# Every projection in three reduced-precision passes, with most of the weight splitting moved to GpSimd

## The chip, the core and the metric

The kernel runs on one core of one Trainium2 chip. The metric is device time in microseconds (us) of one execution. TensorE (PE in the profile) multiplies, VectorE (DVE) and ScalarE (ACT) do elementwise work, GpSimd (POOL) is a slower elementwise engine, SyncE (SP) issues the DMAs. Each engine works through its own instructions in program order and waits on semaphores that the others raise.

## The reference

Two layers of a backbone act on 128 context tokens and 128 latent tokens (width 1024, float32). Cut to what matters here:

```
h = rmsnorm(x) * (1 + scale) + shift                 # adaLN modulation from silu(c) @ w_ada
z = h @ w_in                                         # conv_in, conv_gate, ssm_in, ssm_gate, q, k, v, attn_gate, merge
A) ya = a * sigmoid(g); depthwise conv, 31 taps; layernorm; silu;   br_a = (ya * silu(conv_gate)) @ w_conv_out
B) yb = bidirectional complex state space scan (32 groups, state 64);
   yg = gelu(yb) @ w_ssm_glu; yb = yg_a * sigmoid(yg_b);            br_b = (yb * silu(ssm_gate)) @ w_ssm_out
C) q, k = rmsnorm per head, rotary for the latent tokens; o = softmax(q k / 8) v
                                                                    br_c = (o * silu(attn_gate)) @ w_attn_out
mixed = sigmoid(m_a) * br_a + sigmoid(m_b) * br_b + sigmoid(m_c) * br_c
x = x + gate * (mixed @ w_out)
```

Outputs are both token streams after two layers, the context keys and values of each layer, and the final scan states.

## The kernel before

The two token streams (s = 0 context, s = 1 latent) each fill the 128 partitions. A projection of up to 512 columns is a "unit". Its weights come in slabs of two 128-row tiles (512 KB for 512 columns) through a ring of seven buffers called `raw`, and one slab means 2 streams x 2 tiles = 4 products of 128x128 by 128x512. Units of `w_in`: `cg`, `ssm`, `ca` (early), `q`, `kv` (256 columns), `sg`, `ag` (this group is called the zone here), `gg` (run inside attention), `glub` and `glua` (the state space GLU, inside attention too), the merge gates `meB0` to `meA1`, then branch outputs `brB0` to `brA1` and `wo0`, `wo1`.

A unit is computed in one of two ways. The plain way (`plain_slab`, line 805) multiplies in full float32. The split way (`split_products`, lines 833 to 835) writes a weight as a high part plus a low part in the type fp32r, and does three cheaper products: high by high, high by low, low by high. The high part of a slab (a "piece") is a ScalarE copy of 1024 elements per partition into a spare room (line 1193), the low part is a VectorE subtraction raw - high (`low_parts`, through the helper at line 1477) written back over `raw`. Before the change `cg`, `ssm`, `ca`, all merge, branch and output units are split, and `q`, `kv`, `sg`, `ag`, `gg`, `glub`, `glua` are plain.

The order of the work is written out by hand in `order(l)`, and all engines follow the same list of stages. For each layer, in words:

- early units, then `UT`, `S` (states in, PE L963), `cp` (VectorE computes the scaled matrix CP, 12 operations of 1024 elements), `bbar`, `bz` (GpSimd), the zone units with `K` between them.
- `scan`: VectorE runs 32 dependent steps, each of four additions or products of 128 elements. Behind it on VectorE: `qkn` (squares, norm, rotary of q and k), some convolution taps, then the copies `HY<-H` for which the stage `Y` on PE (L1053, L1055) waits.
- `conv`: 31 x 4 = 124 taps per layer, each one VectorE operation on 256 elements (line 1584), handed out by `TAPS_IN_ZONE`, `TAPS_IN_ATT` and the `conv` stages. The last tap has to be done before `cback` behind the sixth of the merge units (`comb C 0`).
- attention `att 0`, `att 1` with `gg`, `glub`, `glua` pieces between the steps; then six `comb` stages B0, B1, C0, C1, A0, A1, each four merge pieces and two branch pieces; then `wout`.

In layer 0 the stages `comb A` also hold `pre` for the next layer: VectorE computes 12 operations of 1024 elements there (`tA<-lamc,bbar` and the like).

PSUM has four `proj` banks used in turn, so a unit waits until the bank four uses back is drained.

Of the kernel before, what the change touches and what calls it, by code (L numbers as in the profile page):

```python
# [47 lines left out]
EARLY = ("cg", "ssm", "ca")  # L48
LATE_ROOMS = 3
# [6 lines left out]
IN_ATT_UNITS = ("gg", "glub", "glua")  # L56


def order(l):

    def nxt(*stage):
# [4 lines left out]
             ("chunks", "ca", 4), ("pre", 0, 1), ("unit", "ca"), ("taps", 0), ("preE", 0, 0), ("pack",), ("preE", 0, 1)]  # L66
    if l:
# [4 lines left out]
    turn = [] if l else [("bbar", l)]  # L72
    return (begin
            + [("UT",), ("S",), ("cp",)] + turn + [("bz", 0), ("convT", 0), ("convT", 1), ("unit", "q"), ("unit", "kv"),
               ("adaE", l, 2), ("K", 0), ("unit", "sg"), ("bz", 1), ("K", 1), ("unit", "ag")] + nxt("adaE", n, 0)
            + [("scan", 0, NCHUNK), ("qkn",), ("conv", TAPS_IN_ZONE[l], None), ("Y",), ("adaT", l, 2)] + nxt("adaT", n, 0)
            + [("qkT", 0), ("qkT", 1), ("att", 0)] + nxt("adaE", n, 1)
            + [("geT",), ("att", 1), ("unit", "glub"), ("unit", "glua"), ("split", 0), ("split", 1)]
            + nxt("adaT", n, 1)
            + [("brT", "B", 0), ("brT", "B", 1), ("conv", 12, "B0"), ("comb", "B", 0)]  # L80
            + nxt("bT", n) + [("brT", "C", 0), ("brT", "C", 1), ("conv", 12, "B1"), ("comb", "B", 1)]
            + nxt("cT", n) + [("conv", -1, "C0"), ("comb", "C", 0)]
# [47 lines left out]
def stages():  # L130
    out = [(0, s) for s in (("cond",), ("ada", 0, 0, 0, 2), ("small",), ("tabA",), ("mod",), ("ada", 0, 0, 2, DT),
                            ("sq", 0, 0), ("sq", 0, 1), ("xn", 0, 0), ("xn", 0, 1), ("adaE", 0, 0), ("adaT", 0, 0),
                            ("tabS",), ("hT", 0, 0), ("hT", 0, 1), ("early", 0, 0), ("early", 0, 1),
                            ("ada", 0, 1, 0, DT), ("adaE", 0, 1), ("adaT", 0, 1), ("hT", 1, 0), ("hT", 1, 1),
                            ("early", 1, 0), ("chunks", "cg", 1), ("early", 1, 1))]
    for l in range(DEPTH):
        out += [(l, s) for s in order(l)]
    return out
# [16 lines left out]
def split_unit(u):  # L155


    return u[:2] in ("me", "br", "wo") or u in EARLY

# [87 lines left out]
def build(nc, A, C, O):  # L247

    with ExitStack() as ctx:  # L249
# [29 lines left out]
        mixed, mixeds = shared("mixed", [P, NS, D])  # L279
        y2 = mixed[:, :, 0:W]  # L280
        ytok = mixed[:, :, W:D]
        hT = sb("hT", [P, NS, DT, P])
# [7 lines left out]
        pre = sb("pre", [P, 2, 16, L, GC])  # L290
# [3 lines left out]
        tA = sb("tA", [P, 1024])  # L294
        tB = sb("tB", [P, 1024])
        brows = tA[:, :].rearrange("x (p c) -> x p c", p=SP)
        bz = sb("bz", [P, 2, 16, 3 * GC])
        bbar = sb("bbar", [P, 2, G, GC])
# [18 lines left out]
        geT = HYf[:, 0, :].rearrange("p (s t q) -> p s t q", s=NS, t=WT)  # L317
# [15 lines left out]
        th = sb("th", [P, 4, W])  # L333

# [13 lines left out]
        hTs = high_low(Hs, DT)  # L348
# [72 lines left out]
        pieces = [key for key in order_of_slabs if key[0] != "ada" and split_unit(key[1])]  # L421
        piece_at = {key: m for m, key in enumerate(pieces)}
        piece_hi = sem("piece_hi")
        piece_lo = sem("piece_lo")
# [9 lines left out]
        rooms_of = lambda u: early_room if u in EARLY else wout_room if u[:2] == "wo" else late_room  # L434
        piece_room, piece_prev, n_of, last_in = [], [], {}, {}
        for m, (l, u, kp) in enumerate(pieces):
            kind = "early" if u in EARLY else "wout" if u[:2] == "wo" else "late"
            i = n_of.get((l, kind), 0) % len(rooms_of(u))
            n_of[(l, kind)] = n_of.get((l, kind), 0) + 1
            where = ("early" if kind == "early" else "late", i)  # L440
            piece_room.append(rooms_of(u)[i])
            piece_prev.append(last_in.get(where))
            last_in[where] = m

        def piece_slot(m, tile):
            n = KT_SLAB * W * (slab_at[pieces[m]] % RAW)
            return tile[:, n:n + KT_SLAB * W]

        def piece_raw(m):
            return raw[:, slab_at[pieces[m]] % RAW, :]  # L450

        def ahead(l, u, beside=2):

            m = max(i for i, c in enumerate(pieces) if c[:2] == (l, u)) + 1
            room = 0 if m == len(pieces) or (pieces[m][1] in EARLY) != (u in EARLY) else beside
# [8 lines left out]
        for key, _, _, _ in slabs:  # L464
            if key[0] != "ada" and split_unit(key[1]):
# [4 lines left out]
            elif key[0] == "ada":  # L470
                ring = ada_ring(key[:3])
                slab_read.append((ring.full, ring.at[key[:3]][0] + 1))
            else:
                slab_read.append((proj.full, proj.at[key[:2] + (NS - 1,)][0] + 1))
# [12 lines left out]
        split_lo = sem("split_lo")  # L487
# [45 lines left out]
        qk_rs = sem("qk_rs")  # L533
        qk_done = sem("qk_done")
# [45 lines left out]
        for l, stg in todo:  # L580
            if stg[0] in ("split", "brT"):
# [43 lines left out]
        def _(sp):  # L625
# [26 lines left out]
            def b_loads(l):  # L652
                if l:
                    sp.wait_ge(cp_done, 2 * l)
                    sp.wait_ge(bbar_done, l)
                for d in range(2):
                    for r, nm in enumerate(("ssm_b_re", "ssm_b_im")):
                        sp.dma_start(tA[64 * d + 32 * r:64 * d + 32 * r + 32, :],
                                     A[nm][l, d].rearrange("g p c -> g (p c)")).then_inc(b_in, 16)

            def mid_loads(l):
# [3 lines left out]
                if l:  # L665
                    sp.wait_ge(prodA, NS * l)
                    sp.wait_ge(gelu_done, NS * l)
                    sp.wait_ge(qk_done, NS * l)
                    sp.wait_ge(long_.full, long_.at[("pv", l - 1, 1)][0] + 1)
# [7 lines left out]
            def results(l):  # L677
                sp.wait_ge(qk_done, ls(l, 0))
# [81 lines left out]
        def _(pe):  # L760
# [30 lines left out]
            def plain_slab(key):  # L791

                l, u, kp = key
                nk, n = nk_of(u), cols_of(u)
                lhs = geT if u[:2] == "gl" else hT
# [3 lines left out]
                slab_landed(pe, key)  # L799
                w = slab_view(key)  # L800
                for s in range(NS):
                    for i in range(KT_SLAB):
                        kt = KT_SLAB * kp + i
                        last = kt == nk - 1
                        m = T.matmul(proj.bank((l, u, s))[:, 0:n], lhs[:, s, kt, :], w[:, i, :],  # L805
                                     start=(kt == 0), stop=last)
                    if last:
                        m.then_inc(proj.full, 1)
                if not last:
                    m.then_inc(slab_used, 1)  # L810

            def slab_work(key):
                if key[0] == "ada":
                    ada_slab(key)
                else:
                    plain_slab(key)
# [5 lines left out]
            def split_products(l, u, kt, lhs, streams):  # L822
# [4 lines left out]
                part = slice(W * (kt % KT_SLAB), W * (kt % KT_SLAB) + W)  # L827
                pe.wait_ge(piece_lo, m_ + 1)
                whi, wlo = piece_room[m_][:, part], piece_slot(m_, raws)[:, part]
                for s in streams:  # L830
                    bank = proj.bank((l, u, s))
                    hi, lo = (lhs[i][:, s, kt % WT if u[:2] == "wo" else kt, :] for i in range(2))
                    T.matmul(bank[:, :], hi, whi, start=(kt == 0), stop=False)  # L833
                    T.matmul(bank[:, :], hi, wlo, start=False, stop=False)  # L834
# [1257 lines left out]
```

## Time and profile before

| | us |
|---|---|
| median of 3 runs | 714.88 |
| lowest, highest | 713.8, 714.9 |
| the profiled execution | 713.04 |
| its span | 711.0 |
| its mean granted TensorE clock | 0.969 |

Busy time in the span: PE 652.4 us, DVE 551.5, ACT 297.3, POOL 36.4. The span is what the instruction records cover, and the execution's own time is 2.04 us longer. Busy shares are averages; the stage tells which engine holds the others up.

### The profile page before, as it was taken

Reading aid. Unit: us, or ns where it says so; the run is one execution under the profiler, and the core shown is the slowest. Engines: PE = TensorE matmul, PEld = TensorE weight load, DVE = VectorE, ACT = ScalarE, POOL = GpSimd, SP = SyncE. Lnnn points to the kernel's source line nnn. Section 1 sums busy time; section 2 is a strip of 40 time slices with the busy share of each in tenths; the row PEclk is TensorE's granted clock in tenths of the full one; section 3 lists DMA queues with packets and bytes.
Section 4 is the critical chain, followed back from the end, with each engine's and each line's share of the span. In section 5 each row is a group of like instructions: output and inputs, shape, how many; then the busy total and the mean of one; then the engine's idle time right before and its main releaser. Section 6 shows DMA issues by size and latency. Waiting matters only on the chain. (4 is left out here: it accounts for less than half of the span.)

```text
span 711.0 us, 9584 instructions
## 1 busy us (share of the span) xinstructions
PE 652.4 (92%) x3573; PEld 466.5 (66%) x3573; DVE 551.5 (78%) x1024; ACT 297.3 (42%) x454; POOL 36.4 (5%) x49
## 2 busy tenths in 40 slices
PE   3689899996997999998999899999897999999997
PEld 1368674553843688877887687465664578877885
DVE  3679689989777886589975657998878698887663
ACT  2564350212533445435455736011445444436441
POOL 2100001111000000010001010012000000010000
PEclk9989889998998999999999999999998999999999
DMA  8992817654383274654543437660632346655631
GB/s 289 348 275 70 275 36 232 239 183 141 123 272 122 75 229 146 179 176 149 167 158 95 138 136 252 205 240 11 198 112 66 89 121 184 199 165 164 201 104 59
DMA packets 67305, 117.65 MB, mean 165 GB/s; under 512 B 11052, under 2 KB 15484, under 8 KB 67260
## 3 DMA queue, kind: packets, MB, share of 16 engines
q1 hardware_dynamic: 66980, 116.94, 51.9%
q8 instruction: 28, 0.46, 0.3%
q10 hardware_dynamic: 280, 0.11, 0.1%
q14 instruction: 17, 0.14, 0.1%
HBM read 112.51 MB, written 1.38 MB: 160 GB/s over the span
## 5 line engine op out<-in xcount | busy, mean ns | idle before, releaser
L805 PE MATMUL proj<-raw,hT 128*128 128x512 f32 (+1 forms) x320 | 132.0, 558 | 0.0
L1584 DVE SCALAR_TENSOR_TENSOR cvacc<-cvpad,taps,cvacc 128x256 f32<-128x256 f32 x240 | 98.6, 477 | 0.3
L805 PEld LDWEIGHTS proj<-raw,hT 128*128 128x128 f32 x320 | 58.2, 190 | 58.8 <-issue 57.0
L1477 DVE TENSOR_TENSOR raw_split<-raw,wide_split 128x1024 fp32r<-128x1024 f32 x56 | 67.9, 1220 | 21.6 <-ACT wide_split L1193 20.9
L1193 ACT ACTIVATE wide_split<-raw 128x1024 fp32r<-128x1024 f32 x56 | 58.6, 1059 | 55.9 <-PE proj L835 55.9
L834 PE MATMUL proj<-raw_split,H_split 128*128 128x512 f32 x192 | 75.4, 393 | 0.0
L833 PE MATMUL proj<-wide_split,H_split 128*128 128x512 f32 x144 | 57.9, 402 | 4.7 <-DVE raw_split L1477 4.7
L835 PE MATMUL proj<-wide_split,H_split 128*128 128x512 f32 x144 | 56.9, 395 | 0.0
L1477 DVE TENSOR_TENSOR raw_split<-raw,utok_split 128x1024 fp32r<-128x1024 f32 x28 | 34.2, 1220 | 15.1 <-ACT utok_split L1193 15.1
L1193 ACT ACTIVATE utok_split<-raw 128x1024 fp32r<-128x1024 f32 x28 | 29.6, 1058 | 34.8 <-PE proj L835 34.8
L834 PEld LDWEIGHTS proj<-raw_split,H_split 128*128 128x128 f32 x192 | 36.4, 190 | 7.3
L1477 DVE TENSOR_TENSOR H<-H,qkt 128x128 f32<-128x128 f32 x128 | 39.0, 305 | 2.2
L834 PE MATMUL proj<-raw_split,mixed_split 128*128 128x512 f32 x96 | 38.5, 401 | 0.0
L834 PE MATMUL proj<-raw_split,qM_split 128*128 128x512 f32 x96 | 37.5, 391 | 0.0
L833 PEld LDWEIGHTS proj<-wide_split,H_split 128*128 128x128 f32 x144 | 27.5, 191 | 11.9 <-DVE raw_split L1477 4.7
L805 PE MATMUL proj<-raw,HY 128*128 128x512 f32 x64 | 32.4, 653 | 0.0
L835 PEld LDWEIGHTS proj<-wide_split,H_split 128*128 128x128 f32 x144 | 27.4, 190 | 5.9
L1390 ACT ACTIVATE pre<-side,nmx 128x128 f32<-128x128 f32 (+1 forms) x32 | 13.2, 416 | 41.2 <-PE side L820 16.4
L1166 ACT ACTIVATE gates<-proj 128x512 f32<-128x512 f32 x12 | 7.0, 597 | 54.7 <-PE proj L805 54.7
L1053 PE MATMUL side<-qM,Uz 128*64 128x64 f32 x128 | 19.7, 239 | 8.4 <-DVE HY L1908 8.4
L1055 PE MATMUL side<-EC,HY 128*64 128x64 f32 x256 | 25.4, 237 | 0.0
L834 PE MATMUL proj<-raw_split,HY_split 128*128 128x512 f32 x64 | 24.9, 390 | 0.0
(252 smaller groups left out, 1327.0 us busy)
## 6 DMA issues: line engine op xcount, KB each, us to landing
raw<-in_w_in SPq DMA_DIRECT2D x104, 512.0 KB, 4.3
raw<-in_w_ada SPq DMA_DIRECT2D x48, 512.0 KB, 5.3
raw<-in_w_out SPq DMA_DIRECT2D x16, 512.0 KB, 3.8
raw<-in_w_ssm_glu SPq DMA_DIRECT2D x8, 512.0 KB, 7.0
raw<-in_w_ssm_out SPq DMA_DIRECT2D x8, 512.0 KB, 4.3
raw<-in_w_attn_out SPq DMA_DIRECT2D x8, 512.0 KB, 3.7
raw<-in_w_conv_out SPq DMA_DIRECT2D x8, 512.0 KB, 3.7
raw<-in_w_in SPq DMA_DIRECT2D x8, 256.0 KB, 3.7
```

The source lines that it names most:

```text
L805: m = T.matmul(proj.bank((l, u, s))[:, 0:n], lhs[:, s, kt, :], w[:, i, :], start=(kt == 0), stop=last)
L833: T.matmul(bank[:, :], hi, whi, start=(kt == 0), stop=False)
L834: T.matmul(bank[:, :], hi, wlo, start=False, stop=False)
L835: m = T.matmul(bank[:, :], lo, whi, start=False, stop=last)
L1053: T.matmul(o, Uz[:, g, :], M[:, :, g // 2, :], start=True, stop=False)
L1055: m = T.matmul(o, HY[:, q % 2, gi, r, :, :].rearrange("p s k -> p (s k)"), CP[:, r, 1:L + 1, g, :], start=False, stop=(r == 1))
L1166: S.activation(gates[:, GATE[u], s, :], proj.bank(key)[:, :], ACT.Silu).then_inc(proj.freed(key), 1)
L1193: S.activation(piece_room[m], piece_raw(m), ACT.Copy).then_inc(piece_hi, 1)
L1390: m = S.activation(prob[:, p % 2, nk * P * a:nk * P * a + nk * P], side.bank(key)[:, nk * P * a:nk * P * a + nk * P], ACT.Exp, bias=nmx[:, ...
L1477: return V.tensor_tensor(out, a, b, op)
L1584: m = V.scalar_tensor_tensor(acc, src, taps[:, t, j:j + 1], acc, ALU.mult, ALU.add)
```

## The change

All units become split. The low parts are shared out by `low_on_pool`: GpSimd subtracts for the zone units, for the units inside attention, and for the merges B0, B1, C0, A0 and A1; VectorE keeps those of the early units, of C1 and of `wout`. That the activations are now kept as a high and a low copy for the whole layer (`hTe`) removes the `split` stages from attention. Further moves: `bbar` and the norm and rotary of k go to GpSimd, the sums of squares to ScalarE (`sumsq`, 20 small activations a layer), the norm of q into the scale of the exponential, the copies `HY<-H` ahead of q's norm, and convolution taps from the zone and attention to the merges.

```
-def split_unit(u):
-    return u[:2] in ("me", "br", "wo") or u in EARLY
+def low_on_pool(u):
+    return u in ZONE or u in IN_ATT_UNITS or u[2:] in ("B0", "B1", "C0", "A0", "A1")
...
-TAPS_IN_ZONE = (16, 8)
-TAPS_IN_ATT = (((8, 8, 8, 8, 8), (7, 4, 4, 7, 0)), ((6, 6, 6, 6, 6), (7, 4, 4, 7, 0)))
+TAPS_IN_ZONE = (4, 0)
+TAPS_IN_Y = (0, 4, 6)
+TAPS_IN_ATT = (((8, 8, 5, 5, 2), (5, 5, 5, 5, 0)), ((6, 6, 3, 3, 2), (5, 5, 5, 5, 0)))
...
-            + [("UT",), ("S",), ("cp",)] + turn + [("bz", 0), ("convT", 0), ("convT", 1), ("unit", "q"), ("unit", "kv"),
-               ("adaE", l, 2), ("K", 0), ("unit", "sg"), ("bz", 1), ("K", 1), ("unit", "ag")] + nxt("adaE", n, 0)
-            + [("scan", 0, NCHUNK), ("qkn",), ("conv", TAPS_IN_ZONE[l], None), ("Y",), ("adaT", l, 2)] + nxt("adaT", n, 0)
+            + [("UT",), ("S",), ("cp",), ("bz", 0), ("convT", 0), ("convT", 1), ("unit", "q"), ("unit", "kv"), ("adaE", l, 2),
+               ("sumsq", 0), ("K", 0), ("bz", 1), ("unit", "sg"), ("sumsq", 1), ("K", 1), ("scan", 0, NCHUNK), ("HY",),
+               ("unit", "ag")] + nxt("adaE", n, 0)
+            + [("qkn",), ("conv", TAPS_IN_ZONE[l]), ("Y",), ("adaT", l, 2)] + nxt("adaT", n, 0)
...
-            + [("brT", "B", 0), ("brT", "B", 1), ("conv", 12, "B0"), ("comb", "B", 0)]
-            + nxt("bT", n) + [("brT", "C", 0), ("brT", "C", 1), ("conv", 12, "B1"), ("comb", "B", 1)]
-            + nxt("cT", n) + [("conv", -1, "C0"), ("comb", "C", 0)]
+            + [("brT", "B", 0), ("brT", "B", 1), ("conv", 22), ("comb", "B", 0)]
+            + nxt("bT", n) + [("brT", "C", 0), ("brT", "C", 1), ("conv", 22), ("comb", "B", 1)]
+            + nxt("cT", n) + [("conv", -1), ("comb", "C", 0)]
...
                 for m in range(lows[0], upto):
-                    dve.wait_ge(piece_hi, m + 1)
-                    tt_(piece_slot(m, raws), piece_raw(m), piece_room[m].bitcast(F32),
-                        ALU.subtract).then_inc(piece_lo, 1)
+                    if not low_on_pool(pieces[m][1]):
+                        dve.wait_ge(piece_hi, m + 1)
+                        tt_(piece_slot(m, raws), piece_raw(m), piece_high(m).bitcast(F32),
+                            ALU.subtract).then_inc(piece_lo[0], 1)
...
+            def low_parts(upto):            # GpSimd's
+                for m in range(lows[0], upto):
+                    if low_on_pool(pieces[m][1]):
+                        pool.wait_ge(piece_hi, m + 1)
+                        tt_(piece_slot(m, raws), piece_raw(m), piece_high(m).bitcast(F32),
+                            ALU.subtract).then_inc(piece_lo[1], 1)
```

First place, GpSimd from the zone on, layer 0. Before:

```order
L2039 MEMSET bz 128x1536
L2040 COPY bz<-bbar 64x32x16
L2041 COPY bz<-bbar 64x32x16
L2042 COPY bz<-bbar 128x32x16
L2040 COPY bz<-bbar 64x32x16
L2041 COPY bz<-bbar 64x32x16
L2042 COPY bz<-bbar 128x32x16
L2005 TENSOR_SCALAR qst<-qst 128x10
```

The same place with the change (`raw_split<-raw,..._split` is a low part, 1024 elements for a full piece and 512 for one of `kv`):

```order
L2111 COPY bz<-bbar 128x32x16
L2007 TENSOR_TENSOR raw_split<-raw,pre_split 128x1024 x2
L2007 TENSOR_TENSOR raw_split<-raw,gates_split 128x1024
L2007 TENSOR_TENSOR raw_split<-raw,pre_split 128x512 x2
L2007 TENSOR_TENSOR raw_split<-raw,gates_split 128x512
L2007 TENSOR_TENSOR raw_split<-raw,pre_split 128x512
L2007 TENSOR_TENSOR raw_split<-raw,pre_split 128x1024
L2007 TENSOR_TENSOR raw_split<-raw,gates_split 128x1024
L2109 COPY bz<-bbar 64x32x16
```

GpSimd, which had three copies at a time here, now has the low parts of all sixteen zone pieces, twelve full ones and four half ones, around those copies.

Second place, VectorE through the merges B0 and B1, layer 0. Before (a tap is `cvacc<-cvpad,taps,cvacc`):

```order
L1972 SCALAR_TENSOR_TENSOR HY_split<-side,HY_split 128x512 x2
L1584 SCALAR_TENSOR_TENSOR cvacc<-cvpad,taps,cvacc 128x256 x4
L1477 TENSOR_TENSOR raw_split<-raw,wide_split 128x1024
L1584 SCALAR_TENSOR_TENSOR cvacc<-cvpad,taps,cvacc 128x256 x4
L1477 TENSOR_TENSOR raw_split<-raw,wide_split 128x1024
L1584 SCALAR_TENSOR_TENSOR cvacc<-cvpad,taps,cvacc 128x256 x4
L1477 TENSOR_TENSOR raw_split<-raw,utok_split 128x1024
L1477 TENSOR_TENSOR raw_split<-raw,wide_split 128x1024 x2
L1947 SCALAR_TENSOR_TENSOR mixed<-th,proj 128x512
```

With the change, as far as the end of C0's taps:

```order
L1978 SCALAR_TENSOR_TENSOR HY_split<-side,HY_split 128x512 x2
L1609 TENSOR_SCALAR cvacc<-cvpad,taps 128x256 x2
L1612 SCALAR_TENSOR_TENSOR cvacc<-cvpad,taps,cvacc 128x256 x20
L1953 SCALAR_TENSOR_TENSOR mixed<-th,proj 128x512 x2
L1978 SCALAR_TENSOR_TENSOR qM_split<-side,qM_split 128x512 x2
L1612 SCALAR_TENSOR_TENSOR cvacc<-cvpad,taps,cvacc 128x256 x22
L1953 SCALAR_TENSOR_TENSOR mixed<-th,proj 128x512 x2
L1612 SCALAR_TENSOR_TENSOR cvacc<-cvpad,taps,cvacc 128x256 x18
```

The low parts are gone from VectorE's list, and 62 taps stand where 28 stood (74 for 46 in layer 1).

## Rows read from the trace of the kernel before

**Rows 1.** Page, part 1: busy us (share) and instructions.

```profile
PE 652.4 (92%) x3573; PEld 466.5 (66%) x3573; DVE 551.5 (78%) x1024; ACT 297.3 (42%) x454; POOL 36.4 (5%) x49
```

**Rows 2.** Timeline of PE, layer 1's zone: start, us, engine, line.

```profile
457.34 1.99 PE L805 MATMUL proj<-raw,hT 128*128 128x256 f32 x8
...
471.87 14.00 PE L805 MATMUL proj<-raw,hT 128*128 128x512 f32 x32
...
490.36 14.00 PE L805 MATMUL proj<-raw,hT 128*128 128x512 f32 x32
507.34 0.45 PE L1053 MATMUL side<-qM,Uz 128*64 128x64 f32 x2 [2.98 <-DVE HY L1908]
```

**Rows 3.** Timeline of PE, a split unit, twelve products apart.

```profile
596.86 0.39 PE L833 MATMUL proj<-utok_split,H_split 128*128 128x512 f32 x1
...
599.58 0.39 PE L833 MATMUL proj<-wide_split,H_split 128*128 128x512 f32 x1
```

**Rows 4.** Timeline of DVE, layer 1's zone.

```profile
440.96 1.23 DVE L1477 TENSOR_TENSOR tA<-cT,lamr 128x1024 f32<-128x1024 f32 x1
...
455.72 0.29 DVE L1477 TENSOR_TENSOR qkt<-H,lamI 128x128 f32<-128x128 f32 x1
...
490.82 0.83 DVE L1477 TENSOR_TENSOR qkt<-qk 128x640 f32<-128x640 f32 x1 [0.33 <-DVE H L1477]
...
506.17 1.97 DVE L1908 COPY HY<-H 64x1024 f32<-64x1024 f32 x2
```

**Rows 5.** Timeline of DVE, layer 0's zone.

```profile
115.03 1.29 DVE L1477 TENSOR_TENSOR tA<-bbar,coef 128x512 f32<-128x512 f32 x2
...
131.73 0.58 DVE L1477 TENSOR_TENSOR qkt<-H,lamI 128x128 f32<-128x128 f32 x1
...
133.83 0.29 DVE L1477 TENSOR_TENSOR qkt<-H,lamI 128x128 f32<-128x128 f32 x1
```

**Rows 6.** Timeline of POOL: copies beside that scan; a one-element operation.

```profile
131.47 0.69 POOL L2040 COPY bz<-bbar 64x512 f32<-64x512 f32 x1 [9.09 <-PE side L976]
132.22 0.76 POOL L2041 COPY bz<-bbar 64x512 f32<-64x512 f32 x1
133.04 0.61 POOL L2042 COPY bz<-bbar 128x512 f32<-128x512 f32 x1
...
636.14 1.07 POOL L2005 TENSOR_SCALAR st<-st 128x1 f32<-128x1 f32 x1 [5.07 <-DVE st L1919]
```

**Rows 7.** Timeline of DVE at that one-element operation.

```profile
635.97 1.19 DVE L1477 TENSOR_TENSOR raw_split<-raw,wide_split 128x1024 fp32r<-128x1024 f32 x1
```

**Rows 8.** Groups of instructions on POOL by line, shapes apart: busy, mean ns.

```profile
L2014 POOL COPY qk<-ldt 64x128 f32<-64x128 f32 x1 | 0.3, 282 | 9.0 <-DMA ldt<-in_ssm_log_dt 9.0
```

**Rows 9.** Timeline of PE, layer 0: stage Y begins.

```profile
174.93 0.44 PE L1053 MATMUL side<-qM,Uz 128*64 128x64 f32 x2 [5.44 <-DVE HY L1908]
```

**Rows 10.** Timeline of PE, first attention of layer 1.

```profile
522.85 3.60 PE L805 MATMUL proj<-raw,hT 128*128 128x512 f32 x8
...
526.93 3.60 PE L805 MATMUL proj<-raw,hT 128*128 128x512 f32 x8
```

**Rows 11.** Timeline of DVE, there: six taps.

```profile
523.58 2.46 DVE L1584 SCALAR_TENSOR_TENSOR cvacc<-cvpad,taps,cvacc 128x256 f32<-128x256 f32 x6
```

**Rows 12.** Windows: length, busy of PE, PEld, DVE, ACT, POOL, clock, DMA.

```profile
247.00:303.60 56.60, 56.60 (x298) 46.95 (x298) 40.76 (x61) 25.28 (x29) 0.00 (x0) 0.97 0.62 191
...
574.00:624.00 50.00, 49.95 (x224) 41.37 (x225) 45.25 (x75) 22.27 (x25) 0.00 (x0) 1.00 0.59 175
```

**Rows 13.** Windows, PE alone: layer 0's merges A0 and A1.

```profile
324.00:362.00 38.00, 36.04 (x172) 1.00 0.54 163
```

**Rows 14.** Groups on ACT by line: high parts, small evictions.

```profile
L1193 ACT ACTIVATE wide_split<-raw 128x1024 fp32r<-128x1024 f32 x56 | 58.6, 1059 | 55.9 <-PE proj L835 55.9
...
L1377 ACT ACTIVATE wide<-side 48x160 f32<-48x160 f32 x32 | 7.7, 290 | 10.9 <-PE side L976 10.9
```

More of the change, by code:

```diff
@@ L152, in units_of, with kind_of @@
     return []
-def split_unit(u):
-    return u[:2] in ("me", "br", "wo") or u in EARLY
+def kind_of(u):
+    if u in EARLY:
+        return "early"
+    if u in ZONE:
+        return "zone"
+    if u in IN_ATT_UNITS:
+        return "att"
+    return "wout" if u[:2] == "wo" else "late"
+def low_on_pool(u):
+    return u in ZONE or u in IN_ATT_UNITS or u[2:] in ("B0", "B1", "C0", "A0", "A1")
 def side_uses(l, stage):
@@ L464, in build @@
         for key, _, _, _ in slabs:
[L465 removed]
+            if key[0] != "ada":
                 slab_read.append(piece_read[piece_at[key]])
@@ L580, in build @@
         for l, stg in todo:
-            if stg[0] in ("split", "brT"):
+            if stg[0] == "geT":
+                parts += [(l, "geT", s) for s in range(NS)]
+            elif stg[0] == "brT":
                 parts.append((l,) + stg)
@@ L798, in plain_slab @@
                         proj.claim(pe, (l, u, s))
[L799 to L816, printed above, removed]
+                for kt in range(KT_SLAB * kp, KT_SLAB * kp + KT_SLAB):
+                    split_products(l, u, kt, geTs if u[:2] == "gl" else hTe, range(NS))
             def transpose(out, in_):
@@ L1102, in _ @@
                     for u, nk, n in units_of(stg):
-                        if not split_unit(u):
+                        if k == "unit" and u not in EARLY:
                             for key in slab_keys(l, stg):
@@ L1313, in _ @@
                 elif k == "unit" and stg[1] in ("sg", "ag"):
+                    high_parts(ahead(l, stg[1]))
                     gate(l, stg[1])
+                elif k == "sumsq":
+                    s = stg[1]
+                    proj.drained(act, (l, "q", s))
+                    proj.drained(act, (l, "kv", s))
+                    for i in range(HEADS + KV):
+                        h = i // 2 + 4 * (i % 2) if i < HEADS else i
+                        m = S.activation(sq_out[:, s, HD * i:HD * i + HD], qk[:, s, HD * i:HD * i + HD], ACT.Square,
+                                         accum_out=qst[:, s, 0, h:h + 1])
+                    m.then_inc(qk_sq, 1)
                 elif k == "comb":
@@ L2025, in _ @@
                     for s in range(NS):
-                        pool.wait_ge(qk_sq, ls(l, s))
-                        rsqrt_mean(qst[:, s, 2, :], qst[:, s, 0, :], HD, HEADS + KV, qst[:, s, 1, :], qk_rs)
+                        k_norm(l, s)
+                elif k == "UT":
+                    low_parts(piece_at[(l, "q", 1)])
+                elif k == "unit" and stg[1] in ZONE:
+                    low_parts(ahead(l, stg[1]))
+                elif k == "HY":
+                    low_parts(ahead(l, "ag"))
+                elif k == "att":
+                    low_parts(ahead(l, "glua" if stg[1] else "gg"))
+                elif k == "comb":
+                    low_parts(ahead(l, "br" + stg[1] + str(stg[2]), 0))
+                elif k == "bbar":
+                    pool.wait_ge(pre_done, 2 * (l + 1))
+                    pool.wait_ge(tab_done, 1)
+                    if l:
+                        side.filled(pool, ("K", l - 1, 7))
+                    for i in range(2):
+                        side.drained(pool, ("bT", l, i))
+                    co = [coef[:, j, G * l:G * l + G].unsqueeze(2).to_broadcast([P, G, GC]) for j in range(2)]
+                    t0, t1 = (bzf[:, W * i:W * i + W].rearrange("p (g c) -> p g c", g=G) for i in range(2))
+                    b0, b1 = (bbar[:, r, :, :] for r in range(2))
+                    tt_(t0, b0, co[1])
+                    link(tt_(t1, b1, co[1]))
+                    tt_(b0, b0, co[0])
+                    link(tt_(b1, b1, co[0]))
+                    tt_(b0, b0, t1, ALU.subtract)
+                    tt_(b1, b1, t0, ALU.add).then_inc(bbar_done, 1)
                 elif k == "cback":
```

330 lines of the change are left out of this document (175 added, 155 removed).

## The prediction

> **What bounds the kernel now.** I read the busy shares first. TensorE is busy for 92% of the span, VectorE for 78%, ScalarE for 42%, GpSimd for 5% [rows 1]. So TensorE is the first suspect, and GpSimd is nearly free. Then I read TensorE's timeline stage by stage, to see which stages are really its own. In layer 1's zone it runs without a hole from 471.87 to 504.36, then stands for 2.98 us until 507.34, and what releases it is VectorE's copy `HY<-H` [rows 2]. In layer 0 the same hole is 5.44 us, up to 174.93 [rows 9]. VectorE's timeline shows why: the scaled matrix from 440.96, the scan from 455.72 to 490.5, then q's and k's norm, taps, and the copies only at 506.17 [rows 4]. The zone is thus nearly balanced, with VectorE last. In the merges B0 to C0 TensorE is busy all the time: 56.6 of 56.6 us in layer 0 and 49.95 of 50.00 in layer 1, with VectorE at 45.25 of the 50 in layer 1 [rows 12]. Again two engines close together, TensorE ahead.
>
> **What TensorE saves.** Four plain slabs take 14.00 us, so one takes 3.50 [rows 2]. A split slab is twelve products, 599.58 - 596.86 = 2.72 us [rows 3]. That is 0.78 us less per slab, and there are 20 full ones in a layer (q, sg, ag, gg four each, glub and glua two each): 15.6 us. A `kv` slab of 256 columns takes 1.99 us [rows 2]. Split products of that width are not in the trace, and with half of 2.72 they would take 1.36, with no gain at all 1.99. I take 1.4, so 2.4 us for four. Together 18 us a layer, 36 us in all: the profiled execution's 713.04 could become 677 and no less, if everything else kept up.
>
> **What GpSimd's part costs.** The change puts 50 full and 4 half subtractions a layer on GpSimd, which did none. The question is what VectorE does meanwhile. Layer 0's scan shows it: steps take about 1.05 us (34.8 us less the delay below, over 32 steps [rows 4]), but the one that begins at 131.73 takes 2.10 [rows 5], while three GpSimd copies of 512 elements run [rows 6]. 1.05 us over three copies is 0.35 us of delay for each. And the other way: a GpSimd operation on one element, at 636.14, takes 1.07 us and ends just behind VectorE's subtraction of 635.97, which takes 1.19 us [rows 6, 7]. So each holds the other off when both read two SBUF streams or one against two. The Trainium skill says so in "SBUF — State Buffer", section on who shares ports: the pair is an exclusive lock, held for the full instruction, and a VectorE operation with two SBUF inputs contends with a GpSimd one that reads SBUF. The trace agrees on the two cases above. It speaks against this change: every scan step, every tap and the scaled matrix have two SBUF inputs.
>
> How long a subtraction of 1024 elements holds VectorE is not in the trace; call it p. Lower end: counting elements alone, twice a copy's 512 at 0.35, 0.70 us. Scaled by both inputs, 2 x 2 x 0.35 = 1.4. Upper end: four times a copy's own undisturbed 0.61 [rows 6], 2.44. A copy of 128 elements takes 0.282 [rows 8] and one of 512 takes 0.61, so 0.33 us for 384 more, 0.86 ns an element: 2048 elements read make 1.76 us. I take p = 1.76, since it comes from two rows on GpSimd's own rate with the fixed part out, and keep 0.7 and 2.44 for the range. A half piece costs p/2.
>
> The skill has a price for it, in "GPSIMD Engine Reference", section 3.1: a two-input addition of 2048 fp32 elements takes 4497 ns, so as an estimate 2.25 us for 1024. By that price the sum below would be +41 us in place of +8, some 756 us.
>
> **The zone, part by part.** Off VectorE's chain before `Y` go the norm, rotary and taps between 490.5 and 506.17 [rows 4]; they move behind the copies, where `Y` (from 507.34 to about 520) covers them, and the k part to GpSimd. In layer 0 `bbar` goes too: the scan can begin at 115.2 instead of 119.0 [rows 5]. Added on GpSimd beside the scaled matrix and the scan are q2, q3, the four half pieces, sg and ag: ten full and four half, 12p. (TensorE reaches ag at about 482, before the scan ends, so all of them fall inside it.) The `bz` copies are in the measured scan already. From the scan's end to `Y` I take 2.0 us, ScalarE's copy of the forward half. Layer 1: Y at 490.5 + 12p + 2.0 = 492.5 + 21.1 = 513.6 for 507.34 before, **+6.3**. TensorE's own work would be done at 504.4 - 12 x 0.78 - 2.4 = 492.6, so it waits 21 us for the scan. Layer 0: 115.2 + 34.8 + 21.1 + 2.0 = 173.1 for 174.93, **-1.8**.
>
> **Attention.** In layer 1 a step took 4.08 us [rows 10], of which the taps are 2.46 [rows 11]. With five or so taps (2.05) and about 1.05 of reductions and copies VectorE needs 3.1 + p = 4.9, +0.8 for each of four steps. At the end of the first attention twelve taps become two, 10 x 0.41 = 4.1 us less on the chain. In the second the two splits of the activations go, about 1. Together -2 in layer 1; in layer 0 its longer steps (5.3, with two adaLN slabs in each) cover p, so -3. **-5**.
>
> **The merges.** B0, B1, C0 are 18 pieces. VectorE loses 18 subtractions, but has 74 taps in layer 1 (46 before) and 62 in layer 0 (28 before), 0.41 us each by [rows 11], and all need two SBUF inputs. The last tap must precede `cback`, which ends the stage. GpSimd can do three pieces ahead, as there are three rooms, so the two share 15p + 74 x 0.41 + 1.4 (two additions) = 26.4 + 30.3 + 1.4 = 58.1 us where TensorE took 50.0 [rows 12]: **+8.1**. In layer 0: 26.4 + 25.4 + 1.4 = 53.2, hidden under 56.6: 0. While VectorE is late its `mixed` operations free the branch banks late, and that is where TensorE will stand. A0 and A1 in layer 0: 12p + twelve operations of `pre` at 1.23 + 2.8 = 38.6 us against 38.0 [rows 13], so 0. In layer 1 A0 and A1 have no `pre`, and p is below a piece's 2.72: 0.
>
> ScalarE gains 22 full copies at 1.06 us (four of `kv` at half), and 20 sums of squares a layer, by the nearest small operation 0.29 each, 6 us [rows 14]. At 42% busy it has room: 0, or +4 if a copy stands before an exponential.
>
> **Sum** for p = 1.76: +6.3 - 1.8 - 5 + 8.1 = +7.6 us on the profiled execution's 713.04, that is 720.6. That execution lies 1.8 under the median of the runs, 714.88; on the median it is 722.5, and I say 722. The steps move with p by 12 in each zone, 8 in each attention and 15 in layer 1's merges, so some 50 us per us of p, and no change lies at p = 1.6.
>
> **Rivals.**
> - *TensorE's gain comes through.* If GpSimd's reading leaves gaps that VectorE uses (p = 1.4 or less). For it: the delay measured is only 0.35 of a copy's 0.61. Against: two inputs. At 1.4: +2.0 - 6.1 - 8 + 2.7 = -9.4, 705 us. At 0.7: -6.4 - 14.5 - 13 + 0 = -34, 681 us, near the floor of 36.
> - *The lock for the full instruction* at 2.1 to 2.44: layer 1's zone +14.5, layer 0's +6.4, merges +18.3 and +6.8, A0 and A1 +8.7 at the upper end, 770 us; at 2.1 some 745. For it: the one-element operation that waited the whole of VectorE's. It decides above p = 1.6, as the forecast does, only more so. Its place is layer 1's scan: a hole on TensorE of over 25 us.
> - *No difference.* p between 1.55 and 1.65, 712 to 717.
> - *ScalarE sets the pace* in attention and gives 4 to 8 us of a gain back: 710, if p is 1.4. Against it: its idle time there.
>
> **Chances.** Forecast (p 1.65 to 1.95) 0.31, all slower. Full lock 0.19, slower. Gain comes through 0.37, faster; ScalarE rival 0.05, faster. No difference 0.08. A measurement of this kernel tells 0.2% from nothing. So faster 0.42, same 0.08, slower 0.50. The range goes from 686 (p about 0.85) to 746 (p about 2.1). The forecast's own is 715 to 731.
>
> **What would show it.** Slabs of 2.72 us with L847 to L849 in the zone: the saving is there. The GpSimd subtraction's mean, and VectorE's scan: 34.8 us before, about 52 with p = 1.76. The start of `Y` against 507 - 441. TensorE idle before L1053's successor, released by `HY`. Taps whose mean is far above 477 ns in B0 to C0. I am wrong if the scan stays under 45 us, and then the time is near 700; I am wrong the other way if a subtraction takes 2.2 us and all of it is seen in the scan.

## The result, and the profile after

The changed kernel takes 777.5 us (775.8 to 779.7, 4 runs) against 714.3 (709.0 to 714.9, 4 runs): ratio 1.090 [1.084, 1.096], so 9% slower. The forecast was 722 with a range of 686 to 746. Direction right, size wrong. The rival of the full lock (770) comes nearest. The profiled execution took 779.66 us, its span is 777.9.

Page of the changed kernel, busy us by engine, and the chain that ended last; the first row answers to [rows 1]:

```profile
PE 642.9 (83%) x3765; PEld 508.0 (65%) x3765; DVE 619.9 (80%) x936; ACT 348.5 (45%) x578; POOL 340.4 (44%) x189
...
DVE 50%; PE 31%; issue 4%; ACT 4%; SPq 4%; DMA 4%; POOL 2%; ACTq 0%; DVEq 0%; POOLq 0%
```

VectorE has 88 instructions fewer than before and is busy for 68 us more. It now carries half of the chain. TensorE's stages, by the starts of `S`, `Y` and `cback` in both traces (before / after, us):

| stretch | layer 0 | layer 1 |
|---|---|---|
| S to Y | 84.8 / 89.6 | 74.9 / 89.5 |
| Y to cback | 128.9 / 142.3 | 116.7 / 135.2 |
| cback to next S, or end | 128.6 / 143.5 | 86.9 / 88.2 |

TensorE's timeline in layer 1's zone answers to [rows 2]. The first rows open four split slabs; they take 517.26 - 506.02 = 11.24 us, so 2.81 each where a plain one took 3.50. The last is the hole ahead of `Y`, 2.98 us before:

```profile
506.02 0.50 PE L847 MATMUL proj<-pre_split,hTh 128*128 128x512 f32 x1
506.36 0.39 PE L848 MATMUL proj<-raw_split,hTh 128*128 128x512 f32 x1
...
517.26 2.97 PE L990 MATMUL side<-EC,bz 128*48 128x80 f32 x40
...
554.48 0.45 PE L1069 MATMUL side<-qM,Uz 128*64 128x64 f32 x2 [21.16 <-DVE HY L1642]
```

VectorE's timeline there answers to [rows 4]: two instructions of the scaled matrix, the first alone and the second beside GpSimd, the copy ahead of the scan, the first multiplication of the scan, its last additions, and the copies that release `Y`:

```profile
476.19 1.23 DVE L1508 TENSOR_TENSOR HY<-cT,lamr 128x1024 f32<-128x1024 f32 x1
...
479.84 3.30 DVE L1508 TENSOR_TENSOR HY<-cT,lamr 128x1024 f32<-128x1024 f32 x1
...
499.10 2.39 DVE L1852 COPY H<-h 128x128 f32<-128x128 f32 x1
501.52 2.34 DVE L1508 TENSOR_TENSOR qkt<-H,lamI 128x128 f32<-128x128 f32 x1
...
551.62 0.61 DVE L1508 TENSOR_TENSOR H<-H,qkt 128x128 f32<-128x128 f32 x2
...
552.37 1.96 DVE L1642 COPY HY<-H 64x1024 f32<-64x1024 f32 x2
```

The same instruction takes 1.23 us alone and 3.30 beside GpSimd; a multiplication that took 0.29 takes 2.34. From the start of the scaled matrix to the scan's end are 552.2 - 476.2 = 76.0 us, where before 490.5 - 441.0 = 49.5. VectorE's busy time contains this waiting. In layer 0 one such meeting can be read on both engines. VectorE and then GpSimd:

```profile
126.11 0.29 DVE L1508 TENSOR_TENSOR qkt<-H,lamI 128x128 f32<-128x128 f32 x1
...
126.52 2.78 DVE L1508 TENSOR_TENSOR H<-H,qkt 128x128 f32<-128x128 f32 x2
129.34 0.29 DVE L1508 TENSOR_TENSOR qkt<-H,lamI 128x128 f32<-128x128 f32 x1
```

```profile
126.48 2.35 POOL L2007 TENSOR_TENSOR raw_split<-raw,gates_split 128x1024 fp32r<-128x1024 f32 x1 [0.49 <-ACT gates_split L1214]
```

The two additions, 0.61 us otherwise, begin 0.04 us behind the subtraction and end 0.47 behind its end. Groups of the changed kernel, GpSimd's largest, and VectorE's taps and scan additions (477 and 305 ns before):

```profile
L2007 POOL TENSOR_TENSOR raw_split<-raw,wide_split 128x1024 fp32r<-128x1024 f32 x40 | 111.9, 2811 | 59.2 <-ACT wide_split L1214 58.9
```

```profile
L1612 DVE SCALAR_TENSOR_TENSOR cvacc<-cvpad,taps,cvacc 128x256 f32<-128x256 f32 x240 | 157.6, 726 | 0.2
L1508 DVE TENSOR_TENSOR H<-H,qkt 128x128 f32<-128x128 f32 x128 | 56.2, 439 | 2.2
```

Windows of B0 to C0, layers 0 and 1, answer to [rows 12]:

```profile
251.72:321.50 69.78, 61.61 (x303) 50.05 (x301) 52.04 (x76) 26.05 (x31) 41.91 (x16) 0.90 0.55 165
624.35:689.65 65.30, 53.88 (x226) 43.38 (x225) 65.09 (x85) 23.92 (x27) 42.96 (x16) 0.92 0.49 145
```

In layer 1 VectorE is busy for 65.1 of 65.3 us: it sets the pace, where TensorE did. The granted clock fell from 1.00 to 0.92, and the low stretches lie behind TensorE's new waits.

### The profile page after: what moved, and what is told of

It is laid out like the page before. It is cut to its first block, busy times and chain, and to the rows that moved or that the text cites. A ratio compares the mean times of both kernels' runs of the same rounds, so it can differ in the third digit from the quotient of the medians.

```text
span 777.9 us, 10189 instructions
## 1 busy us (share of the span) xinstructions
PE 642.9 (83%) x3765; PEld 508.0 (65%) x3765; DVE 619.9 (80%) x936; ACT 348.5 (45%) x578; POOL 340.4 (44%) x189
## 4 chain that ended last, share of the span: by engine, by line
DVE 50%; PE 31%; issue 4%; ACT 4%; SPq 4%; DMA 4%; POOL 2%; ACTq 0%; DVEq 0%; POOLq 0%
DVE cvacc L1612 15%; DVE qkt L1508 7%; PE proj L847 7%; DVE H L1508 7%; PE proj L849 6%; PE proj L848 6%; DVE HY L1508 6%; DMA raw<-in_w_in 3%; PE side L833 3%; PE side L1071 2%; DVE EC L1508 1%; PE side L977 1%; DVE H L1792 1%; SPq L724 1%; PE side L1069 1%
## 5 line engine op out<-in xcount | busy, mean ns | idle before, releaser
L848 PE MATMUL proj<-raw_split,hTh 128*128 128x512 f32 (+1 forms) x448 | 175.1, 391 | 0.0
L1612 DVE SCALAR_TENSOR_TENSOR cvacc<-cvpad,taps,cvacc 128x256 f32<-128x256 f32 x240 | 157.6, 726 | 0.2
L2007 POOL TENSOR_TENSOR raw_split<-raw,wide_split 128x1024 fp32r<-128x1024 f32 x40 | 111.9, 2811 | 59.2 <-ACT wide_split L1214 58.9
L848 PEld LDWEIGHTS proj<-raw_split,hTh 128*128 128x128 f32 x448 | 86.3, 193 | 15.6
L847 PE MATMUL proj<-wide_split,hTh 128*128 128x512 f32 x144 | 61.1, 424 | 9.9 <-POOL raw_split L2007 7.1
L2007 POOL TENSOR_TENSOR raw_split<-raw,pre_split 128x1024 fp32r<-128x1024 f32 (+1 forms) x20 | 48.7, 2443 | 39.8 <-ACT pre_split L1214 39.8
L849 PE MATMUL proj<-wide_split,hTl 128*128 128x512 f32 x144 | 59.3, 412 | 0.0
L2007 POOL TENSOR_TENSOR raw_split<-raw,utok_split 128x1024 fp32r<-128x1024 f32 x20 | 53.8, 2692 | 2.0 <-ACT utok_split L1214 1.9
L847 PE MATMUL proj<-gates_split,hTh 128*128 128x512 f32 (+1 forms) x112 | 45.1, 402 | 6.4 <-DVE raw_split L1508 4.4
L849 PE MATMUL proj<-gates_split,hTl 128*128 128x512 f32 (+1 forms) x112 | 43.0, 384 | 0.0
```

The costliest lines, as they stand in the source:

```text
L847: T.matmul(bank[:, 0:n], hi, whi, start=(kt == 0), stop=False)
L848: T.matmul(bank[:, 0:n], hi, wlo, start=False, stop=False)
L849: m = T.matmul(bank[:, 0:n], lo, whi, start=False, stop=last)
L1612: m = V.scalar_tensor_tensor(acc, src, taps[:, t, j:j + 1], acc, ALU.mult, ALU.add)
L2007: return Q.tensor_tensor(out, a, b, op)
```

## The experiments

Three theories. **T1, sharing:** a GpSimd subtraction holds VectorE off for its length. **T2, supply:** GpSimd is just too slow for TensorE. **T3, order:** the moved taps, the order and ScalarE's added work. All times are medians; the kernel before took 713.0 to 714.3 in every group.

**GpSimd writes and reads nothing.** The subtraction at line 2021 becomes

```
slot = piece_slot(m, raws).bitcast(F32)
link(Q.memset(slot, 0.0))
link(Q.memset(slot[:, 0:W], 0.0))
Q.memset(slot, 0.0).then_inc(piece_lo[1], 1)
```

> In place of each subtraction GpSimd writes zeros into the same slot two and a half times over: no input is read, the duration stays near that of a subtraction (about 2.4 us). The low parts are left out of the result; nothing else changes. Theory 1 (a GpSimd instruction with two inputs in SBUF holds off VectorE's instructions of the same sort for its whole length): the time falls from 777 to about 690 (680 to 705), the scan of layer 0 from 50.9 to about 35 us, a tap from 726 to about 480 ns. Theory 2 (GpSimd is too slow to feed TensorE, 2.4 to 2.8 us a piece against 2.7): stays at 770 to 780. Theory 3 (the moved taps, the order and the added work on ScalarE): stays at 770 to 780.

The short form keeps only the last write.

> In place of each subtraction GpSimd writes zeros into the slot once, about 0.9 us; the low parts are left out of the result. Theory 1: within 8 us of the kernel with the long writes (about 685). Theory 2: clearly below the kernel with the long writes, near 700, while that one stays near 775. Theory 3: both near 775.

Measured: 704.4 us with the long writes, 702.5 with the short. So 73 of the changed kernel's 777.5 us go by taking away GpSimd's reads at the same length of work (0.95 + 0.53 + 0.96 us for the 2.43 of a subtraction). Making that work 1.5 us shorter for each piece gives about 2 more, inside the scatter of the short form (699.0 to 706.4). T2 is out, and T3 alone cannot explain it. The writes also leave TensorE zeros to multiply by. That this is not what gives the time back is seen in VectorE's rows below, and in the granted clock, 0.97 here and in the kernel before, which multiplies by real low parts. The page of the kernel with long writes, and its chain; VectorE is busy for 154 us less with the same 936 instructions:

```profile
PE 628.5 (90%) x3765; PEld 499.5 (71%) x3765; DVE 465.9 (66%) x936; ACT 348.5 (50%) x578; POOL 313.5 (45%) x405
...
PE 64%; ACT 8%; DMA 7%; DVE 7%; SPq 6%; issue 4%; POOL 3%; ACTq 0%; DVEq 0%; POOLq 0%
```

Its groups: taps and scan are back at the old means.

```profile
L1612 DVE SCALAR_TENSOR_TENSOR cvacc<-cvpad,taps,cvacc 128x256 f32<-128x256 f32 x240 | 97.5, 479 | 0.2
L1508 DVE TENSOR_TENSOR H<-H,qkt 128x128 f32<-128x128 f32 x128 | 38.3, 299 | 2.2
```

The time lies inside the expected 680 to 705, but 14 us above the 690 at its centre. That is a loss of its own, taken up below.

**Where the sharing costs.** Long writes for one group of pieces only (`kind_of(...) == "late"`, and the reverse).

> The changed kernel, GpSimd writing zeros in the same time in place of the subtractions of the merges alone (those low parts are left out of the result); in the zone and the attention it subtracts. Theory 1: of the 73 us between the changed kernel and the one with writes alone, the merges' part comes back: B0 to C0 of layer 1 from 65 to 50 us, 777 to about 735 (730 to 745). If the zone carries the loss: 760 or more.

> The other half: writes in place of the subtractions of the zone and the attention (those low parts are left out of the result), subtractions in the merges. Theory 1: the zones' part comes back, 777 to about 745 (735 to 755), the scans at 35 us. The two parts should add up to about 73 us if the stages are independent.

Measured: 740.5 (37.0 us back) and 747.0 (30.5 back), together 67.5 of the 73. T1's expectations hold for both, and the stages are nearly independent. With writes in the merges alone, TensorE's windows of B0 to C0 are:

```profile
249.37:310.45 61.08, 57.21 (x303) 47.15 (x301) 34.37 (x78) 26.07 (x31) 39.11 (x49) 0.97 0.65 194
601.93:651.91 49.98, 49.98 (x228) 41.42 (x226) 38.97 (x87) 22.89 (x26) 39.45 (x49) 1.00 0.59 176
```

Layer 1 is back at its old 50.0 us. Layer 0 keeps 4.2 us over the 56.9 from its first product to `cback` before, so there the sharing cost 8.7 of 12.9.

**The price by itself, in the kernel before.** In GpSimd's program, beside the scan:

```
+ if k == "scan":
+     pool.wait_ge(h0_done, l + 1)
...
+     for n in range(6):
+         tt_(spare, x[:, 0, :], x[:, 1, :], ALU.subtract).then_inc(beside, 1)
+         pool.wait_ge(beside, 6 * l + n + 1)
```

`spare` is a buffer that is free then, and the last line makes each one wait for the one before it.

> The kernel before, with six subtractions of 1024 elements on GpSimd in each layer beside the scan (two inputs in SBUF, output into a buffer that is free then); no result uses them. Theory 1 (a GpSimd instruction with two inputs holds VectorE's instructions of this sort off for its whole length): each costs the scan about 2.0 to 2.4 us, the scan of layer 0 grows from 35.9 to 48 to 50 us, the kernel by 15 to 28. The prediction's price of 1.76: 10.6 us a scan, at most 20. Theory 2 or 3: nothing, 713.

> The same six places with a copy of 1024 elements, one input in SBUF (about 1.2 us each). Theory 1, if what counts is the two inputs: the scan grows by less than 1 us. Rival (any GpSimd instruction that reads SBUF holds VectorE off for its length): 6 x 1.2 = 7 us a scan, kernel up by 7 to 14.

> The same six places with a write of zeros of 1024 elements, no input (0.9 us each). Theory 1: scan unchanged, 713. Rival (sharing by any access): 6 x 0.9 = 5 us a scan.

Measured: 741.1, 723.1 and 712.2 us. The scans (35.88 and 34.77 us before) took 48.74 and 47.66 beside the subtractions, 40.64 and 39.52 beside the copies, 35.91 and 34.80 beside the writes. So a subtraction costs 2.14 and 2.15 us, a copy 0.79 each time, a write 0.01 at most. Theory 1 holds for the subtraction. For the copy my form of it (only two inputs count) failed: one read input is enough. The rival's 7 to 14 us for the kernel was right (9.3), its 7 us a scan was too much (4.8). VectorE's timeline of the first:

```profile
134.55 2.36 DVE L1478 TENSOR_TENSOR qkt<-H,lamI 128x128 f32<-128x128 f32 x1
136.83 0.28 DVE L1478 TENSOR_TENSOR qkt<-H,lamR 128x128 f32<-128x128 f32 x1
137.04 4.88 DVE L1478 TENSOR_TENSOR H<-H,qkt 128x128 f32<-128x128 f32 x2
141.95 2.44 DVE L1478 TENSOR_TENSOR qkt<-H,lamI 128x128 f32<-128x128 f32 x1
```

GpSimd's groups of the first and of the second kernel:

```profile
L2003 POOL TENSOR_TENSOR cvacc<-x 128x1024 f32<-128x1024 f32 x12 | 29.2, 2432 | 0.8
```

```profile
L2018 POOL COPY cvacc<-x 128x1024 f32<-128x1024 f32 x12 | 13.2, 1098 | 0.6
```

The reader is to see turns: the first multiplication waits for one whole GpSimd instruction, the two additions for two (4.88). The second multiplication, `lamR`, passes in 0.28 us. It needs no result of its forerunner, but that alone does not save it, as two rows of the changed kernel show:

```profile
510.93 2.39 DVE L1508 TENSOR_TENSOR qkt<-H,lamI 128x128 f32<-128x128 f32 x1
513.24 2.48 DVE L1508 TENSOR_TENSOR qkt<-H,lamR 128x128 f32<-128x128 f32 x1
```

There GpSimd's next subtraction begins at 513.13, ahead of `lamR` at 513.24, and `lamR` waits 2.2 us for it. Above, each subtraction waits for the one before it, and the next begins at 136.84, together with `lamR`. In these rows, the one that is clearly ahead goes first, and `lamR` passes where both begin together.

**Cut in four.** In the changed kernel `for j in range(0, o.shape[-1], 256)` around the subtraction of each piece; in the old one 24 subtractions of 256 elements in place of the six.

> The changed kernel with each subtraction of 1024 elements on GpSimd as four of 256. If what a subtraction costs VectorE is its whole length however it is cut: 777 within 3 us. If the two engines take turns instruction by instruction, then VectorE gets an instruction in between each two quarters (0.6 us) and waits a quarter of the time for each: 745 to 765, the scan of layer 0 at 42 to 47 us in place of 50.9.

> The kernel before with 24 subtractions of 256 elements a layer beside the scan, in place of six of 1024 (741 us). Whole length however it is cut: 741 within 2 us. Turns by instruction: the scan grows by less than the 12.5 us of the six long ones, by 7 to 10; the kernel at 728 to 735.

Measured: 778.2 in the changed kernel (no change), 736.6 in the old (741.1 uncut). There the scan took 47.87 and 46.73 us, 12.0 over before in both layers, for 24 quarters of 0.776 us: 0.50 each, 2.0 for four against 2.14 uncut. VectorE gets an instruction in between, but the quarters' own time grows: four of 0.776 are 3.1 us against 2.43. In the changed kernel a quarter takes 0.83 to 0.94 us, and the scans grew to 53.5 and 54.2 us where turns were to give 42 to 47. Its stages moved both ways, `Y` to `cback` of layer 1 from 135.2 to 128.4 us and the last stretch from 88.2 to 96.5; why was not looked into. The first theory's number was right for the changed kernel; for the old one neither was (it asked for 741 within 2, the other for a scan 7 to 10 longer).

**The merges' subtractions on VectorE.** `low_on_pool` without B0 to A1, and behind every fourth tap `low_parts(lows[0] + 1)`, as before; then only A0 and A1.

> The subtractions of all merges (B0, B1, C0, A0, A1) go back to VectorE, those of B0 to C0 between its taps as in the kernel before; the zone's and the attention's stay on GpSimd. Theory 1: the merges B0 to C0 of layers 0 and 1 go back to 56 and 50 us (from 69 and 65) and the stretch after them gives 8: 777 becomes about 740 (735 to 750). Theory 2: the merges are slow because GpSimd feeds them late; 745 to 765. Theory 3: no more than 5 us, 772.

> Only the subtractions of A0 and A1, the third branch's, go back to VectorE. Theory 1: the stretch from the end of C1 to A0 in layer 0 loses its 8 us, but VectorE takes 16 subtractions of 1.2 us a layer back: 768 to 775. Theory that these were covered (the step of the prediction that put the third branch at nothing): within 2 us of 777.

Measured: 768.9 and 771.2. The first missed its 735 to 750. Its trace shows why: my edit left the first low parts of B0 behind all 22 taps, since the counter still stood at pieces that are GpSimd's, and TensorE waited 12.1 us. TensorE's timeline there:

```profile
625.13 0.77 PE L847 MATMUL proj<-wide_split,hTh 128*128 128x512 f32 x1 [12.14 <-DVE raw_split L1508]
```

So it was repeated with the counter moved on: `while lows[0] < end and low_on_pool(...): lows[0] += 1`.

> As the kernel with the merges' subtractions on VectorE (769 us), but with the first ones of B0 truly between the taps: there all 21 to 22 taps came ahead of B0's first subtraction, and TensorE waited 12.1 us for it in layer 1. Theory 1: the wait goes. By the prediction's own formula with VectorE's 1.22 us a piece, B0 to C0 of layer 1 take 18 x 1.22 + 74 x 0.41 + 1.4 = 53.7 us against 65.3 with GpSimd; 745 to 757. If a subtraction costs VectorE the same on either engine: 765 to 770.

Measured: 754.8 us, 22.7 less than changed. Y to `cback` falls from 142.3 to 133.3 us in layer 0, from 135.2 to 128.0 in layer 1. Theory 1 holds. The second kernel of the pair held its expectation (6.3 us from A0 and A1 alone), so these were not covered.

**The taps.** The kernel before's tap tables and its 12 and 12 ahead of B0 and B1, first on the faulty kernel, then on the mended one.

> The kernel with the merges' subtractions on VectorE (769 us), and besides it the kernel before's own distribution of the filter taps: more in the zone and the attention, 12 and 12 before B0 and B1 in place of 22 and 22. Theory 1 alone (only the sharing counts, not the order): 769 or more, since more taps then lie beside GpSimd's subtractions. Theory 3 (what the merges lose is VectorE's order, the moved taps): B0 to C0 of layer 1 goes back to 50 us, the kernel to 750 to 760.

> The same mend in the kernel that also has the old distribution of the taps (776 us). Theory 1 alone: no better than the kernel with the new distribution and the same mend, since a tap in the zone or the attention lies beside GpSimd's subtractions and one in the merges now beside none. Theory 3 (the moved taps cost the merges their time): 5 us or more below it.

Measured: 776.5 against 768.9, and 768.2 against 754.8. Both times worse, by 8 and 13 us. T3's part on the moved taps is refuted: later taps were a gain. The mended pair shows where. With the old tables the stretch from `Y` to B0 holds 34 more taps in layer 0 and 26 more in layer 1 and is 11.1 and 6.8 us longer, and B0 to C0 gives back no more than 2.1. The taps' mean there hardly rises in layer 0 (510 to 519 ns) and falls in layer 1 (708 to 585), so what they cost is in the main their own time on the chain, not the sharing.

**Everything on VectorE.** The zone's subtractions between the steps of the scan, the attention's between the heads.

> The changed kernel with every subtraction on VectorE: those of the zone between the steps of the scan, those of the attention between the heads, those of the merges between the taps; GpSimd takes none. Theory 1 (one on GpSimd costs VectorE about twice what its own does, 2.4 against 1.22 us): below 769, the kernel with the merges alone on VectorE, at 735 to 755. Theory 2 (GpSimd too slow a supplier): about the same, 740 to 760. Theory that GpSimd's subtractions are mostly covered: VectorE's 30 more of 1.2 us a layer would cost, 790 or more.

Measured: 771.9, outside 735 to 755. The first layer's scan there goes from 123.6 to 188.6 us, 65.0 long, with VectorE idle for up to 5.41 us ahead of a subtraction whose high part ScalarE has not made yet. So the order of this run costs more than the sharing that it takes away. It doesn't speak against T1, but neither for it.

**ScalarE's queue.** In the changed kernel TensorE waits 4.59 us ahead of layer 1's `S`. ScalarE's timeline:

```profile
459.29 1.06 ACT L1214 ACTIVATE gates_split<-raw 128x1024 fp32r<-128x1024 f32 x1 [10.32 <-DMA raw<-in_w_in]
460.25 1.89 ACT L1369 ACTIVATE HY<-wide 64x2048 f32<-64x2048 f32 x1
```

The high part of q's first piece stands 10.32 us for its slab, and the copy that packs U, ready earlier, stands behind it. The edit at line 1308: `high_parts(piece_at[(l, "q", 0)] + 1)` without the `+ 1`.

> The changed kernel, with ScalarE's high part of q's first piece taken after the copy that packs U (HY<-wide), not ahead of it. In the changed kernel TensorE waits 4.6 us for that copy ahead of S in layer 1, where the kernel before had no such wait. If the queue on ScalarE is the cause: the wait goes and the kernel gains 3 to 5 us (773). If the copy is late for its own transfer (wide<-utok): nothing.

> The same edit in the kernel with the short writes (0.9 us each, low parts left out of the result; 702.5 us), where nothing else hides it: 697 to 699 if the queue on ScalarE is the cause, 702 if not.

Measured: 766.3 (11.2 less) and 694.1 (8.4 less), more than the 3 to 5 expected. ScalarE's timeline of the first shows the copy waiting only for its own transfer:

```profile
447.18 1.92 ACT L1369 ACTIVATE HY<-wide 64x2048 f32<-64x2048 f32 x1 [4.05 <-DMA wide<-utok]
```

More than half of the gain, 6.3 us, lies between layer 0's `cback` and layer 1's `S`, and part at the start of layer 0: TensorE's waits for `EC` copies, behind the same high part, of 2.35 and 1.59 us are gone, and `S` begins at 87.33 in place of 89.67.

**Both mends.**

> Both mends together: the merges' subtractions between the taps on VectorE, and ScalarE's packing copy ahead of q's first high part. If they add (11 us for the second): 734 to 746, still above the kernel before.

Measured: 744.0 us, 10.8 under the first mend alone: they add. It is the fastest kernel with all of the computation in it, and still 4.4% slower than before (ratio 1.044 [1.040, 1.047]). No variant here beats the kernel before; the 694 us leave the low parts out.

## Why the prediction was wrong, step by step

**Bounds now.** Right: nearly balanced, VectorE last in the zone. That is what made the price decide.

**The price p** is the step that failed. I took 1.76 us, the element rate with the fixed part out; measured are 2.14 and 2.15 in the old kernel and, in the changed one's layer 1, 76.0 - 49.5 = 26.5 us over 12 pieces, 2.21. About 1.1 us of the 26.5 is the norm and rotary of k, which GpSimd now does beside the scan and which I had put at nothing; without it a piece costs 2.12. The rows shown before would have told it: a copy of 0.61 us had cost 0.35, so all but 0.26 [rows 6]. Nearly the same difference stands in every later case: 1.10 - 0.79 = 0.31 for the copy of 1024, 2.43 - 2.14 = 0.29 for the subtraction, 0.776 - 0.50 = 0.28 for a quarter. That is about the length of one VectorE instruction of the scan (0.28), which gets in between, and it does not grow with GpSimd's elements. So the loss is GpSimd's whole duration less some 0.3, and its fixed part belongs to it. By that, my own upper end of 2.44 gives p = 2.18.

The Trainium skill says in "SBUF — State Buffer", section "Who interferes with whom", that the shared ports are an exclusive lock and the second to issue waits for the whole instruction; that was the right reading, and the rows above agree. Half of the 4497 ns in "GPSIMD Engine Reference", section 3.1, an estimate of 2.25 us, is near the 2.35 to 2.43 us of a subtraction beside the scan here.

**Four of the formulas held with p = 2.21.** The first is no test, since 2.21 is taken from that stretch. From the start of the scaled matrix to `Y`, layer 1 took 66.4 us before; my steps give +11.7, measured 554.5 - 476.2 = 78.3, +11.9. B0 to C0 of layer 1: 15 x 2.21 + 74 x 0.41 + 1.4 = 64.9, measured 65.3. A0 and A1 of layer 0: 12 x 2.21 + 14.8 + 2.8 = 44.1, +6.1, measured +6.7 (44.6 us from meA0's first product to the last of the branch, 37.9 before); the 6.3 us of the run with A0 and A1 alone on VectorE agree. I had put them at 0. Layer 0's `Y`: 152.0 + 26.5 = 178.5, measured 179.2 and not -1.8 but +4.3.

**Steps wrong beside p.** ScalarE was put at 0 to 4 and cost 11.2: I counted its busy time and not what queued behind an instruction that waits for a slab. Layer 0's B0 to C0 were put at 0 and cost 12.9; my formula with p = 2.21 explains 3.3 (59.9 against 56.6), and the run with writes in the merges puts 8.7 to the sharing and 4.2 to something else. That fits a wait of TensorE of 4.78 us for the fourth piece of B0, whose slab came late to ScalarE. TensorE's and ScalarE's rows:

```profile
266.53 0.79 PE L847 MATMUL proj<-wide_split,hTh 128*128 128x512 f32 x1 [4.78 <-POOL raw_split L2007]
```

```profile
259.49 1.06 ACT L1214 ACTIVATE wide_split<-raw 128x1024 fp32r<-128x1024 f32 x1 [6.90 <-DMA raw<-in_w_in]
```

The wait was not tried apart. Attention was put at -5 and gave +3.6.

**TensorE's saving** was put at 36 us. A slab of the zone fell to 2.81, not 2.72, one of `kv` to 1.69, not 1.4, and TensorE's busy time by 652.4 - 622.4 = 30 us in the kernel with short writes and the mended queue, whose page shows:

```profile
PE 622.4 (90%) x3765; PEld 495.2 (72%) x3765; DVE 466.3 (67%) x936; ACT 348.4 (50%) x578; POOL 158.6 (23%) x189
```

That kernel was 20 us under before. In the changed one TensorE's busy time fell by only 9.5. Its granted clock is lower where it waits, as the windows from `S` to `Y` of layer 1 show, first of the changed kernel, then with long writes (0.86 against 0.98, with 66.1 busy us against 64.8 for the same products):

```profile
465.00:554.70 89.70, 66.08 (x458) 53.62 (x459) 83.64 (x152) 36.77 (x93) 47.26 (x34) 0.86 0.42 141
```

```profile
436.60:506.60 70.00, 64.83 (x459) 52.29 (x460) 60.45 (x157) 39.38 (x95) 43.65 (x58) 0.98 0.41 131
```

**The sum.** My steps with p = 2.21 give +11.7 and +3.6 for the zones, -1.4 for attention, +14.9 and +3.3 for the merges, +6.1 for A0 and A1: +38, 753 us. ScalarE's queue adds 11, attention's miss 5, layer 0's merges 10: 779, measured 777.5. This sum is put together from the measured stages after the fact, and its parts may overlap a little; it shows where the time lies and is no test of its own.

**What would show it.** The mark I set for "wrong the other way" was met: a subtraction of over 2.2 us and nearly all of it seen in the scan, 50.9 us in layer 0. The taps average 726 ns over all, 800 and 812 in the merges. "Slabs of 2.72" was not met, 2.81. The rival of the full lock held in mechanism; it had 0.19 and deserved the place of the forecast. That its 770 was only 1% off is partly luck: its p of 2.44 is above the measured one and adds 17 us to the 753, about what it lacks in ScalarE's queue (11 us) and the rest of layer 0's merges.

What stays open: why that slab of layer 0 lands late, what the 5 us of attention are, and how well the zone's subtractions would do on VectorE in a good order.

## What to carry to other kernels

Before moving elementwise work to GpSimd, take the instruction's own full duration and charge it to VectorE, less about one short VectorE instruction, wherever VectorE is on the chain and works on two inputs in SBUF; here 2.1 to 2.2 us for what VectorE does itself in 1.22. A row in which two engines already meet gives the rule (duration minus what was lost), not a rate to scale by elements. And when an engine gets an early operand to prepare, ask what stands behind it in its queue while it waits for the transfer.

## What the runs showed of the hardware

- A GpSimd copy with one SBUF input holds off VectorE's two-input instructions as well (0.79 of 1.10 us); a GpSimd write of zeros of 0.95 us doesn't at all (scan 35.91 against 35.88).
- VectorE's one-input copy of 128 elements waits too: 2.39 us beside a subtraction, 0.22 without (layer 1, long writes).
- Which of the two waits went by which began first: `lamR` waits for a subtraction that begins 0.11 us ahead of it (513.13 and 513.24), and passes where the two begin within 0.01 us (136.83 and 136.84, subtractions in the old kernel). Two VectorE instructions that need nothing of each other can thus pay twice, 2.39 and 2.48 us.
